# Two layers written out with tokens in two halves around each norm, and the modulation read by rows

## The reference, cut to what matters

```
# first block
sh1, sc1, g1, sh2, sc2, g2 = split(silu(c) @ w_mod + b_mod, 6)      # 1024 -> 6 x 1024
csh1, csc1, ...            = split(silu(c_ctx) @ w_mod + b_mod, 6)
hc = rmsnorm(ctx, norm1_g) * (1 + csc1) + csh1
hx = rmsnorm(x,   norm1_g) * (1 + sc1)  + sh1
... projections of hc and hx with w_in; pooling; gated linear attention
x = x + g1 * mixer_out(...)
x = x + g2 * moe(rmsnorm(x, norm2_g) * (1 + sc2) + sh2)              # 32 experts
x = rmsnorm(x, final_norm_g)
# second model, l = 0, 1
h = rmsnorm(x, g_mix_pre[l])
... = split(h @ w_in[l]); three mixers give o_a, o_b, o_c
x = x + rmsnorm(concat(o_a, o_b, o_c) @ w_out[l], g_mix_post[l])
h = rmsnorm(x, g_ffn_pre[l])
x = x + rmsnorm((gelu(gate) * val) @ w_down[l], g_ffn_post[l])       # gate, val: causal conv of h @ w_up[l]
```

## Time and profile before

| | |
|---|---|
| median of 3 runs | 1978.96 us (1978.42 to 1980.64) |
| profiled execution: its own time | 1978.16 us |
| profiled execution: span from first to last instruction | 1976.1 us |
| PE busy | 1840.6 us, 93% |
| DVE, ACT, GpSimd busy | 651.7, 278.0, 67.0 us |
| mean granted clock of PE | 0.955 |

### The profile page before, as it was taken

One profiled execution on the slowest core, in us unless ns is written; L12 is line 12 of the kernel. 1 busy time (PEld: TensorE's weight loads), 2 busy tenths in 40 slices (PEclk: granted clock), 3 DMA queues, 4 the chain that ended last, 5 costly groups with the idle time before them and its releaser, 6 DMA issues. The chain is left out here.

```text
span 1976.1 us, 21525 instructions
## 1 busy us (share of the span) xinstructions
PE 1840.6 (93%) x9139; PEld 1383.6 (70%) x9139; DVE 651.7 (33%) x1270; ACT 278.0 (14%) x405; POOL 67.0 (3%) x68
## 2 busy tenths in 40 slices
PE   6899999989999999997998998999969998899997
PEld 4545888864554454454888877888858887788886
DVE  3585343121111111112177513442024574234401
ACT  1003122020000000001122221000011322100001
POOL 3000000000000000000003100000000130000000
PEclk8798999989999999999899999999979999999998
DMA  8572322636999999994431122543123302234440
GB/s 302 213 261 80 128 86 96 230 145 272 426 429 426 428 428 426 429 427 166 143 136 43 43 86 95 161 154 145 64 104 128 128 1 86 86 128 149 149 149 22
DMA packets 119132, 375.39 MB, mean 190 GB/s; under 512 B 6154, under 2 KB 55538, under 8 KB 106640
## 3 DMA queue, kind: packets, MB, share of 16 engines
q1 hardware_dynamic: 118032, 373.59, 49.4%
q0 software_dynamic: 1024, 0.69, 0.2%
HBM read 373.22 MB, written 1.05 MB: 189 GB/s over the span
## 5 line engine op out<-in xcount | busy, mean ns | idle before, releaser
L514 PE MATMUL PS<-arena,ring 128*128 128x256 f32 (+2 forms) x3408 | 766.4, 388 | 6.7 <-DVE arena L1940 3.4
L514 PEld LDWEIGHTS PS<-arena,ring 128*128 128x128 f32 (+1 forms) x3408 | 641.6, 189 | 126.3 <-issue 30.5
L791 PE MATMUL PS<-ring,arena 128*64 128x512 f32 x1024 | 225.1, 593 | 8.3 <-DMA ring<-in_moe_w_dram 7.2
L791 PEld LDWEIGHTS PS<-ring,arena 128*64 128x64 f32 x1024 | 74.2, 137 | 156.0 <-issue 156.0
L1137 PE MATMUL PS<-arena,ring 128*128 128x256 f32 x704 | 152.3, 379 | 0.0
L1137 PEld LDWEIGHTS PS<-arena,ring 128*128 128x128 f32 x704 | 133.8, 190 | 18.2
L822 PE MATMUL PS<-ring,arena 128*64 128x512 f32 x512 | 113.4, 595 | 0.5 <-ACT arena L1387 0.5
L1969 DVE TENSOR_SCALAR arena<-PS,col 128x256 f32<-128x256 f32 x112 | 49.1, 479 | 186.1 <-PE PS L514 185.8
L1971 DVE SCALAR_TENSOR_TENSOR arena<-PS,col,arena 128x255 f32<-128x255 f32 (+2 forms) x248 | 108.1, 478 | 4.4
L514 PE MATMUL PS<-ring,arena 128*128 128x512 f32 (+4 forms) x392 | 103.0, 412 | 4.1 <-DMA ring<-in_w_in_dram 1.7
L514 PEld LDWEIGHTS PS<-ring,arena 128*128 128x128 f32 x392 | 66.6, 212 | 40.2 <-issue 35.5
(11 more groups left out here) (341 smaller groups left out, 1292.2 us busy)
## 6 DMA issues: line engine op xcount, KB each, us to landing
ring<-in_moe_w_dram SPq DMA_DIRECT2D x96, 2048.0 KB, 16.5
ring<-in_w_in_dram SPq DMA_DIRECT2D x23, 2048.0 KB, 8.0
ring<-in_ffn_w_up_dram SPq DMA_DIRECT2D x44, 1024.0 KB, 6.8
ring<-in_w_mod_dram SPq DMA_DIRECT2D x12, 2048.0 KB, 12.9
ring<-in_ffn_w_down_dram SPq DMA_DIRECT2D x10, 2048.0 KB, 8.8
ring<-in_w_out_dram SPq DMA_DIRECT2D x4, 2048.0 KB, 7.8
ring<-in_w_gla_br_dram SPq DMA_DIRECT2D x2, 2048.0 KB, 8.5
ring<-in_w_o_dram SPq DMA_DIRECT2D x2, 2048.0 KB, 8.2
```

The source lines that it names most:

```text
L514: last = mm(PS[:, b, place] if not isinstance(place, tuple) else PS[place[0], b, place[1]], lhsT(k), rhs(k), start=(k == 0), stop=(k == K ...
L791: last = mm(PS[e * SLOTS:(e + 1) * SLOTS, 4 + j, :], hg[:, k, e * SLOTS:(e + 1) * SLOTS], expert_slab(2 * j + e, KT)[:, k, :], start=(k == ...
```

## The change

**Modulation by rows.** `w_mod` is read in 24 pieces of 1 MB, each 128 rows of 2048 columns (8 KB in one run of memory). The two vectors, with 30 columns of zeros, are the stationary tile of 128x32; four matmuls of 128x512 for each piece write to four groups of 32 partitions of bank 0. Three groups of 2048 columns; group 0 is needed before `k`. ACT copies the row, PE transposes it, DVE adds the bias. DVE's `mod_sum` and PE's `modulation_sums` are gone. The vectors' loads move from SP's to ACT's queue, most of the constants are loaded later, and phase 1 has 7 banks in place of 8.

**Layers written out.** No loop, no `meet` between and after the layers; semaphores count on (`due`), slabs of layer 1 are issued as soon as ring slots are free, per-layer columns are read in place.

**Halves.** Around each norm, matmuls are done for tokens 0 to 127 and 128 to 255 apart (`th(t)`), with 128 moving columns, and the sums of squares and the norm of one half stand between work on the other. The result too is transposed and written in halves.

```diff
-            def modulation(j):
-                b = ph1.bank(pe, ("mod", j))
-                w = slab("mod", j)
-                for f in range(4):
-                    for k in range(KT):
-                        last = mm(PS[:, b, 2 * f:2 * f + 2], w[:, k, f * P:(f + 1) * P], csil[:, k, :],
-                                  start=(k == 0), stop=(k == KT - 1))
-                last.then_inc(psum_full, 1)
+            def modulation(g, ks):
+                for k in ks:
+                    src, arrived, count = mod_place(g, k)
+                    if g and k == 0:
+                        pe.wait_ge(S("mod_added"), g)
+                    pe.wait_ge(arrived, count)
+                    for j in range(4):
+                        last = mm(PS[32 * j:32 * (j + 1), 0, :], csil[:, k, :], src[:, j * 512:(j + 1) * 512],
+                                  start=(k == 0), stop=(k == KT - 1))
+                    last.then_inc(S("mod_read"), 1)
+            def modulation_turned(g):
+                pe.wait_ge(S("mod_row"), g + 1)
                 for f in range(4):
+                    last = nc.tensor.transpose(PS[:, 0, f * P:(f + 1) * P], mrow[:, f * P:(f + 1) * P], C("ident"))
...
-            with pe.Fori(0, LAYERS) as L:
+            for l in range(LAYERS):
+                ph3.layer = l
...
+                out_unit(0, 0)
+                out_unit(0, 1)
+                bs = ph3.bank(pe, ("middle_sums", 0))
+                out_unit(1, 0, lambda: half_sums(bs, 0, fsq, 0, when_new("sq_f", 1)))
+                out_unit(1, 1, lambda: half_sums(bs, 1, sc3, 0, when_new("sq_x2", 1)))
...
-                square_sums("ms1", fsq, {2 * g: stage("sq_f", g + 1) for g in range(4)})
-                square_sums("ms2", sc3, {0: stage("sq_x2"), 4: stage("sq_x2", 2)})
...
+                for j in range(2):
+                    for v in range(2):
+                        early.append((ph3.bank(pe, ("up", j, v)), j, v))
+                        up_part(*early[-1], 0)
+                        if (j, v) == (0, 0):
+                            half_sums(bs1, 0, fsq, 1, when_new("sq_f", 3))
+                        elif (j, v) == (1, 0):
+                            half_sums(bs1, 1, sc3, 1, when_new("sq_x2", 3))
+                for b, j, v in early:
+                    up_part(b, j, v, 1)
...
+                for f in range(KT):
+                    down_part(f, 0)
+                bt1 = ph3.bank(pe, ("end_sums", 1))
+                for f in range(KT):
+                    if f % 2 == 0:
+                        pe.wait_ge(S("first_copied"), due("first_copied", f // 2 + 1))
+                    down_part(f, 1)
+                    if f == 0:
+                        half_sums(bt, 0, fsq, 0, when_new("sq_f", 5, 2))
+                    if f == 5 and l + 1 < LAYERS:
+                        half_sums(bt, 1, sc3, 0, when_new("sq_x2", 5))
+                    if f == 6 and l + 1 == LAYERS:
+                        for g in range(2):
+                            out_turned(0, g, b_out[g])
...
+                tail_sums = [lambda b=bt1, r=when_new("sq_f", 9, 2): half_sums(b, 0, fsq, 1, r),
+                             lambda b=bt1, r=when_new("sq_x2", 7): half_sums(b, 1, sc3, 1, r)]
```

More of the change, by code:

```diff
@@ L70, in constants @@
         "ones": np.ones((P, P)),
+        "eps": np.full((P, 1), EPS),
+        "one": np.ones((P, 1)),
         "incl": same & (r <= c),
@@ L881, in turn @@
                 last.then_inc(psum_full, 1)
-            with pe.Fori(0, LAYERS) as L:
+            for l in range(LAYERS):
+                ph3.layer = l
                 h = lambda k: hT[:, k, :]
-                square_sums("ms0", sc3, {})
+                if l == 0:
+                    b = ph3.bank(pe, "ms0")
+                    for k in range(KT):
+                        last = mm(PS[:, b, half(0)], C("ones"), sc3[:, k, :], start=(k == 0), stop=(k == KT - 1))
+                    last.then_inc(psum_full, 1)
                 w = slab3("b", n=BQI0 - AB0)
@@ new lines, in bk_part @@
+                def bk_part(b, t):
+                    for i in range(2):
+                        c0 = BK0 - AB0
+                        for k in range(KT):
+                            last = mm(PS[i * 64:i * 64 + 64, b, th(t)], w[:, k, c0:c0 + 64], ready[t](k),
+                                      start=(k == 0), stop=(k == KT - 1))
+                    if t:
+                        last.then_inc(psum_full, 1)
+                b_ab = ph3.bank(pe, "ab")
+                token_part(b_ab, 0, 8, 0, 0, False)
@@ L1411, in _ @@
             v2 = lambda v: v.rearrange("p (j t) -> p j t", j=2)
-            with act.Fori(0, LAYERS) as L:
-                link = Chain(act, "act_step")
+            link = Chain(act, "act_step")
+            for l in range(LAYERS):
+                ph3.layer = l
                 def rs3(view, n, key, width=T):
@@ new lines, in add_normed @@
+                        V.tensor_tensor(xT[:, 4 * i:4 * i + 4, th(t)], xT[:, 4 * i:4 * i + 4, th(t)],
+                                        fT[:, 4 * i:4 * i + 4, th(t)], ALU.add).then_inc(S("x_new"), 1)
+                for t in range(TT):
+                    add_normed(2 * t + 1, "g_mix_post_2", t, lambda k: PS[:, ph3.place(("out", t, k // 4)), th(k % 4)],
+                               lambda k: ("out", t, k // 4) if k % 4 == 3 else None)
+                    dve.wait_ge(S("x_new"), due("x_new", 2 * t + 2))
+                    dve.wait_ge(S("rs_ready"), due("rs_ready", 2 * t + 2))
+                    norm("g_ffn_pre_2", t, l)
```

671 lines of the change are left out of this document (393 added, 278 removed).

## The result

| | before | after |
|---|---|---|
| median | 1979.7 us (4 runs) | 1904.24 us (4 runs, 1902.39 to 1908.27) |
| profiled execution, own time | 1978.16 us | 1904.51 us |
| span | 1976.1 us | 1902.7 us |
| PE busy | 1840.6 us | 1813.8 us |
| mean granted clock of PE | 0.955 | 0.978 |

The ratio is 0.9622, 95% interval 0.9605 to 0.9639: 75 us faster. The direction was right, and so were most of the mechanisms; the sum of the terms was 16 us too small.

The account below looks back on a forecast made before the run. The prediction took PE, busy 93% of the span, as the bound: its work, gaps and half clock. Terms -29.5 + 12 - 10 - 23 - 7 + 0.4 = -57 gave 1922 us; own range 1910 to 1932, 8 in 10 within 1907 to 1940.

Parts of the forecast that it names:

- the term of the modulation: Work behind projection k, up to krc: column-tile passes and transposes added, one-column sums removed; +12 us, bounds +8.5 to +24.
- Layer 0's start: First slab of layer 0: keeps its meeting and 1.6 MB load; cut matmuls cost 0.4 us.
- Start: Everything ahead of projection k: k starts at 38.5 instead of 68.13, -29.5 us, bounds -34 to -26.
- Middles: From w_out to the up projection in each layer: waits covered by halves, -5.0 us a layer, -10 in both.
- Between the layers: From layer 0's w_down into layer 1: 27.6 us gap and 4.5 of half clock go, sums and cuts remain; -23 us.
- End: From the last w_down to the output: 9.4 us to the last issue against 17.3; -7 us.
- Pairs: Rival, modulation's column tiles: they overlap only in pairs, 28.4 us in place of 16.7, total 1934 us; 12%.
- Halves too thin: Rival, middles and layer join: halves cannot hide the chain, 2 us at each place, 16 in all, 1938 us; 14%.
- Half the start: Rival, ahead of k: PE's own work stays slow, k starts at 53, total 1936 us; 9%.
- The clock in the cut work: Rival, cut passes in both layers: the granted clock falls to half, total 2113 us, slower; 3%.
- the join: The stretch between layer 0's w_down and layer 1's first slab, where the prediction put -23 us.

## Why the prediction was wrong in its size

**The step that failed** is the term of the modulation, +12 with bounds +8.5 and +24; it measured +5.3, outside its bounds. Its mechanism held: four column tiles overlap. The 128 passes took 14.4 us (0.113 each, 16.7 predicted at 0.13). The transposes took 1.0 (1.8 predicted), since each is one pass, not two. The changes between full and column tiles cost little: a tile of v between two blocks takes 7.06 us, one without 6.97 (13.93/2), some 0.5 us in all. The removed sums were 7.0 (7.5 predicted). What I had not counted was the clock: z at 9.0 us in place of 12.0 and v 0.7 faster, against 0.85 more in k, whose first 5 us run at half clock. With 0.2 less in q these parts add up to +5.3. The z of this execution is at the low end of what the versions show (9.0 to 11.4); with the longest of them the term would be +7.8, still outside.

The Trainium skill ("TensorEngine Tiling (Array Packing)", Key Properties) says that a mode change drains the engine; by the trace such a drain is below 0.1 us here. The estimate of 0.135 a pass from the Trainium skill's "TensorE: Matmul & The Clock Gate" (Measured speedup vs the span model) was too high; the trace has 0.113.

**Layer 0's start** failed as well: the prediction had it keep "its meeting and its load of 1.6 MB" at a price of 0.4 for the cut, and left out that DVE's steps and PE's order change there too. It gave 4.2. I had counted 4.5 us of half clock for layer 1, where the same first slab stands, and had not looked at the window of layer 0. Two versions place 2.3 of it with DVE's steps and 1.3 with PE's order.

**Start**: -27.4 for -29.5, just inside its bounds. What stands ahead of k was right, what sets its start was not: I had PE's own work and the chain behind it at 38.5, and it was the loads, at 339 to 394 GB/s between 8 and 32 us where I had counted 385 to 427.

**Middles**: -6.6 a layer for -5.0. The cut is what was mis-sized. Counted from start to start, a pass of 128 columns takes 0.112 us (between the sums of the middle 7.15/64) and one of 256 takes 0.216, so a cut matmul costs 0.015 us more, not 0.026: 1.9 a layer for 3.3. With 7.15 for sums and 1.26 for the longer wait the terms give a gain of 16.8 - 7.15 - 1.9 - 1.26 = 6.5, and nothing of size is open. The chain fits: from sum to last square 5.2 us (6.5 predicted) under 7.1 of `w_out`. The Trainium skill's figure of 0.107 us for a weight load of 128 columns ("TensorE: Matmul & The Clock Gate", LDWEIGHTS) would have made the cut free; the trace lies between it and my figure. (By the prediction's own prices a free cut is worth 6.6 + 1.7 + 1.2 + 0.4, some 10 us, not the 8 given there.)

**Between the layers**: -25.9 for -23. The mechanism is as laid out, without a pause above 0.4 us, and the clock was worth more than I had counted. From its first pass to aq layer 1's slab takes 47.45 us before and 41.2 now without the two sums in it. That is 6.2 less although the cut costs 0.5 there, so about 6.7 against my 4.5. The windows show why: before the change 10 us at 0.55 and then the thin passes ahead of aq at 0.81 (4 columns) and 0.50 (64 rows), now 1.00 up to and in the first and 0.57 in the second. The cut's price explains another 0.5. **End**: -6.7 for -7, the second issue 8.7 us behind `w_down` (9.4 predicted).

**The rivals.** Pairs: no, 0.12 a pass. Halves too thin: no, no wait at any of the sums. Half the start: no. The clock in the cut work: no, 1.00 in every window of it. But the experiments show what hangs on the second: a first half without cover costs 19 us, one pause at the join 12.

**The range** was too narrow below because I widened it by the rivals, which all lie above the forecast, and gave the clock a price in one place only. Of the 16 us missed, stretches of z, v, layer 0's and layer 1's start that no longer run slow are some 10, with 0.85 lost in k.

Not tried: the layers written out without halves, so how the join's gain divides between the meeting and the first half's cover stays open. Not shown either: why the clock falls where it does in z and in the thin passes ahead of aq, where the same code takes from 9.0 to 11.4 us and from 5.7 to 8.4.

## What to carry to other kernels

Look at the granted clock behind every pause and every stretch of thin passes in the profile of before, not only where the change was meant to act: here a pause of 3.5 us cost 10, and the clock's share was as large as some terms of the sum. Ask what else an edit changes on the engine that feeds PE: steps of half the size on DVE were worth 2.3 us. When two versions differ by a few us, compare them piece by piece in the trace, since a stretch with the same code in both can differ by 2 us and hide or feign the effect. And keep small loads out of a stretch that is bound by large ones.

## What the runs showed that I had not expected

- With 30 small loads (0.69 MB) beside the large transfers the DMA engines, full in both cases, move 345 GB/s, without them 419. Moved away they brought k forward by 4.7 us, nearly three times what their bytes explain.
- Four column tiles of 32 overlap at 0.113 to 0.12 us a pass, in runs of two or of four passes on a tile, against 0.44 for one alone; changing between them and full tiles costs under 0.1 us.
